# Two blocks on one core: shifted projections and output products in wide banks, the shift's mixing split over two engines, and sums moved

## The chip, the core and the metric

The kernel runs on one core of one Trainium2 chip. The metric is the device time of one execution in microseconds (us), lower is better. TensorE is PE in the rows, VectorE is DVE, ScalarE is ACT, GpSimd is POOL, SyncE is SP.

## The reference

Two blocks of two layers each run on 256 tokens of 1024 features, all in float32. Every layer is a feed-forward network, a mixer, and a second network. The change touches the mixers of the first block, and the place where every mixer hands over to its second network:

```python
h = rms_norm(x, mix_norm[layer])
p = h @ w_in
p_b = p[..., 4096:]
p_b = p_b + mu * (prev(p_b) - p_b)
r, k, v, w_down, a_down = split(p_b)
decay = f(w0 + tanh(w_down) @ w2)
a = sigmoid(a0 + a_down @ a2)
y_a = gated_spatial(p); y_b = time_mix(r, k, v, decay, a)
merged = sigmoid(gate_a) * (y_a @ w_proj_a) + sigmoid(gate_b) * (y_b @ w_proj_b)
x = x + merged @ w_out
```

Here prev(p) is p one token earlier, with zeros ahead of the first token.

## The kernel before

**Products.** Features lie on the 128 partitions, tokens (256) along the free axis. Each float32 operand is split into a high and a low part, and a product takes three terms: high by high, high by low, low by high. There are two forms. The narrow form (`three`, L2030 to L2034) issues three matmuls of 256 columns into one half of a PSUM bank of 512. The wide form (`unit_tiles`, L2122 to L2140) issues one matmul of 512 columns (the high weights against both parts of the activations, which lie side by side) and one of 256. It gives each tile a whole bank, whose two halves must then be added: ScalarE copies one half out, and VectorE adds the other. The networks use the wide form. The shifted projections and the output product of a mixer use the narrow one (`two_tiles`, L2036).

**Weights.** They come in units of 2048 columns, one DMA each, and a unit is 16 weight tiles, that is two halves of 8. ScalarE writes the high part of each half (L928), VectorE the low part (L1342). Both do so in `keep_ahead(w)`, called at fixed places of their programs: it splits all halves up to w + 3. There are four slots, so half m waits until TensorE is through with half m - 4.

**Order.** Each engine runs a program written out by hand, strictly in the order of its code, and waits on semaphores. `mixed` counts finished shift units, `emptied` the banks that ScalarE or VectorE have read, `tanh_ready` and others do what their names say. `bank_for` (L2019) hands out three narrow banks (`lin`, in rotation); `sv` has five more.

**The shift units.** In `rwkv(l)` a mixer starts with 13 units s = 0 to 12, each two tiles of p_b: the pair for decay and a (unit 0, tile `lora`), eight pairs of r and k, four pairs of v. The first two work on rough activations that are not normalized yet (`first_tiles`); the rest use h. For unit s:

- TensorE forms the products in a narrow bank.
- ScalarE calls `keep_ahead(base + 2 * s + 1)` and, from unit 2 on, copies the bank to `raw_shift` (L1068), which has two slots; for units 0 and 1 VectorE does that and scales by `rstd` (L1554). At s = 1 ScalarE also takes the tanh of `lora` (L1072), at s = 10 and 11 squares of the keys `kk` (L942).
- VectorE calls the same `keep_ahead`, then computes diff = prev - p (L1560) and p + mu * diff for each of the two tiles (L1569); from unit 9 on it also scales two tiles of keys into `kk` (L1574).

**After them.** TensorE forms z = tanh(w_down) @ w2 in four banks of `sv` (L2230), then a in four narrow banks (L2236). VectorE adds w0 to each bank of z into `decay` (L1581), ScalarE takes sigmoids of `decay` (L1079) and of a (L1083). A narrow bank can be taken again when the one three uses earlier is emptied. Then come the sums of the keys' squares (L2357) and the units of v_a and u_a.

**The end of a mixer.** Four output units d = 0 to 3 add to x (`residual`, L1516). While they run, ScalarE squares the finished parts of x (L942) and VectorE adds the first three of these into one (`add_squares`, L1379). TensorE turns them into the mean with matmuls against a constant (`norm_sums`, L2154): sum 0 right behind unit d = 3, sum 3 inside the first unit of the network, ahead of its tile k = 4.

## Time and profile before

| | us |
|---|---|
| median of 3 runs (lowest, highest) | 2853.32 (2848.67, 2853.98) |
| the profiled execution | 2854.39 |
| its span | 2852.7 |
| TensorE busy | 2771.2 (97%) |
| VectorE busy | 2127.5 (75%) |
| ScalarE busy | 1569.8 (55%) |
| share of the chain that ended last: TensorE, VectorE, ScalarE | 83%, 9%, 4% |

The profiled execution's own time is 1.7 us over its span, and 1.1 us over the median. Of a busy time it must be kept in mind that matmuls overlap: one of 256 columns is shown with 280 ns, while the next starts 120 ns after it. The start of one instruction to the start of the next is what a product costs. The granted TensorE clock was 0.995 of full speed over the whole span.

### The profile page before, as it was taken

To read this page: it belongs to the slowest core of one execution; us is meant where nothing else is said; L and a number is where in the kernel's file an instruction comes from. 1 tells how busy PE (TensorE), PEld (TensorE's weight loads), DVE (VectorE), ACT (ScalarE), POOL (GpSimd) and SP (SyncE) were. 2 spreads that over 40 slices of the span, in tenths; PEclk is the share of its full clock that TensorE was granted. 3 is DMA by queue.
4 is the path that set the end of the run, shared out by engine and by line. 5 is a ranking of instruction groups with operands and counts; after the bars stand their busy time and mean duration, and the time that the engine had idled before them with its cause. 6 is when DMAs were issued, how large, how long until landed. Compare 5 with 4: busy or idle time off the path is not lost.

```text
span 2852.7 us, 53213 instructions
## 1 busy us (share of the span) xinstructions
PE 2771.2 (97%) x22404; PEld 2469.4 (87%) x22404; DVE 2127.5 (75%) x3171; ACT 1569.8 (55%) x2377; POOL 13.8 (0%) x23
## 2 busy tenths in 40 slices
PE   7999999999999999999999999999999999998999
PEld 7889888898888898788988888888888879998888
DVE  7877667678788787666787798667878776777864
ACT  6545644455556455544465565576546546676653
POOL 0000000000000000000000000000000000000000
PEclk9999999999999999999999999899999999999999
DMA  6675311246757753111557567433675664332454
GB/s 232 250 280 179 131 46 47 88 162 227 266 211 253 286 180 133 61 46 46 193 202 260 203 246 259 178 119 128 249 269 212 246 234 165 146 134 104 163 183 142
DMA packets 72910, 510.62 MB, mean 179 GB/s; under 512 B 8480, under 2 KB 9248, under 8 KB 11872
## 3 DMA queue, kind: packets, MB, share of 16 engines
q1 hardware_dynamic: 72672, 507.22, 49.0%
q8 instruction: 177, 2.90, 0.4%
q14 instruction: 61, 0.50, 0.0%
HBM read 506.13 MB, written 1.05 MB: 178 GB/s over the span
## 4 chain that ended last, share of the span: by engine, by line
PE 83%; DVE 9%; ACT 4%; issue 2%; DMA 1%; SPq 0%; DVEq 0%; ACTq 0%
PE solve_banks L2135 13%; PE solve_banks L2198 11%; PE linear_banks L2135 7%; PE solve_banks L2136 7%; PE solve_banks L2199 6%; PE linear_banks L2032 5%; PE linear_banks L2033 4%; PE linear_banks L2034 4%; PE linear_banks L2136 4%; PE linear_banks L2587 3%; DVE split_halves L1342 3%; PE linear_banks L2588 3%; PE linear_banks L2589 3%; DMA raw_units<-in_stream 1%; PE solve_banks L2449 1%
## 5 line engine op out<-in xcount | busy, mean ns | idle before, releaser
L1342 DVE TENSOR_TENSOR split_halves<-raw_units,split_halves 128x1024 fp32r<-128x1024 f32 x806 | 971.9, 1221 | 315.8 <-ACT split_halves L928 313.2
L928 ACT ACTIVATE split_halves<-raw_units 128x1024 fp32r<-128x1024 f32 x806 | 841.4, 1054 | 437.1 <-PE solve_banks L2199 176.7
L2135 PE MATMUL solve_banks<-h_split,split_halves 128*128 128x512 f32 x1664 | 586.5, 397 | 1.4 <-DVE split_halves L1342 1.3
L2198 PE MATMUL solve_banks<-hidden_split,split_halves 128*128 128x512 f32 x1408 | 498.3, 398 | 0.6 <-DVE hidden_split L1452 0.6
L2136 PE MATMUL solve_banks<-h_split,split_halves 128*128 128x256 f32 x1664 | 465.5, 280 | 0.0
L2199 PE MATMUL solve_banks<-hidden_split,split_halves 128*128 128x256 f32 x1408 | 395.6, 281 | 0.0
L2135 PEld LDWEIGHTS solve_banks<-h_split,split_halves 128*128 128x128 f32 x1664 | 312.3, 188 | 77.5 <-issue 2.0
L2198 PEld LDWEIGHTS solve_banks<-hidden_split,split_halves 128*128 128x128 f32 x1408 | 264.7, 188 | 66.2 <-DVE hidden_split L1452 0.9
L2135 PE MATMUL linear_banks<-h_split,split_halves 128*128 128x512 f32 x896 | 317.3, 397 | 1.4 <-DVE split_halves L1342 1.0
L2136 PEld LDWEIGHTS solve_banks<-h_split,split_halves 128*128 128x128 f32 x1664 | 313.9, 189 | 0.0
L2032 PE MATMUL linear_banks<-h_split,split_halves 128*128 128x256 f32 x864 | 262.1, 303 | 5.7 <-DVE split_halves L1342 4.8
L2199 PEld LDWEIGHTS solve_banks<-hidden_split,split_halves 128*128 128x128 f32 x1408 | 264.3, 188 | 0.1
L2136 PE MATMUL linear_banks<-h_split,split_halves 128*128 128x256 f32 x896 | 250.8, 280 | 0.0
L2033 PE MATMUL linear_banks<-h_split,split_halves 128*128 128x256 f32 x864 | 244.8, 283 | 0.0
L2034 PE MATMUL linear_banks<-h_split,split_halves 128*128 128x256 f32 x864 | 244.4, 283 | 0.0
L2587 PE MATMUL linear_banks<-split_halves,h_split 128*128 128x256 f32 (+1 forms) x784 | 229.2, 292 | 9.6 <-DVE h_split L1421 9.4
L2588 PE MATMUL linear_banks<-split_halves,h_split 128*128 128x256 f32 (+1 forms) x784 | 224.0, 286 | 0.0
L2589 PE MATMUL linear_banks<-split_halves,h_split 128*128 128x256 f32 (+1 forms) x784 | 223.8, 286 | 0.0
L2135 PEld LDWEIGHTS linear_banks<-h_split,split_halves 128*128 128x128 f32 x896 | 168.2, 188 | 42.5 <-issue 2.1
L1446 DVE CUSTOM_DVE_ANT_0 raw_units<-raw_units,condition_rows,modulation 128x1024 f32<-128x1024 f32 x144 | 184.7, 1282 | 5.8 <-DMA raw_units<-in_mod_w 2.9
L2032 PEld LDWEIGHTS linear_banks<-h_split,split_halves 128*128 128x128 f32 x864 | 165.2, 191 | 18.8 <-issue 8.2
L2136 PEld LDWEIGHTS linear_banks<-h_split,split_halves 128*128 128x128 f32 x896 | 169.0, 189 | 0.0
(336 smaller groups left out, 4872.0 us busy)
## 6 DMA issues: line engine op xcount, KB each, us to landing
raw_units<-in_stream SPq DMA_DIRECT2D x403, 1024.0 KB, 4.8
raw_units<-in_mod_w SPq DMA_DIRECT2D x72, 1024.0 KB, 6.0
x<-in_x SPq DMA_DIRECT2D x4, 256.0 KB, 4.2
w2a<-in_w2a SPq DMA_DIRECT2D x2, 512.0 KB, 6.0
w_rows<-in_w SPq DMA_DIRECT2D x2, 512.0 KB, 8.0
bs_rows<-in_bs SPq DMA_DIRECT2D x2, 512.0 KB, 8.5
spatial_t<-in_ws_t SPq DMA_DIRECT2D x2, 512.0 KB, 10.4
out<-x SPq DMA_DIRECT2D x4, 256.0 KB, 4.3
```

What stands on the lines that cost most here:

```text
L928: nc.scalar.activation(split[:, n % SPLIT_SLOTS, 0, :], raw[:, item % RAW_SLOTS, (n % 2) * HALF * P:(n % 2 + 1) * HALF * P], ACT.Copy).the ...
L1342: V.tensor_tensor(split[:, n % SPLIT_SLOTS, 1, :], raw[:, item % RAW_SLOTS, (n % 2) * HALF * P:(n % 2 + 1) * HALF * P], split[:, n % SPLIT ...
L2032: M(o, w_hi, a_hi, start=start, stop=False, skip_group_check=skip)
L2033: M(o, w_hi, a_lo, start=False, stop=False, skip_group_check=skip)
L2034: return M(o, w_lo, a_hi, start=False, stop=stop, skip_group_check=skip)
L2135: M(pairs(banks[:, e, :]), s[:, 0, t], h[:, :, k, :], start=k == 0, stop=False)
L2136: ins = M(banks[:, e, 0:T], s[:, 1, t], h[:, 0, k, :], start=False, stop=k == DT - 1)
L2198: M(pairs(bank), s[:, 0, t], hidden[:, :, k, :], start=k == 0, stop=False)
L2199: ins = M(bank[:, 0:T], s[:, 1, t], hidden[:, 0, k, :], start=False, stop=k == FT - 1)
L2587: M(o, a_hi, s[:, 0, m], start=(c == 0 and j == 0), stop=False, skip_group_check=True)
L2588: M(o, a_lo, s[:, 0, m], start=False, stop=False, skip_group_check=True)
L2589: ins = M(o, a_hi, s[:, 1, m], start=False, stop=(c == DT - 1 and j == NCH - 1), skip_group_check=True)
```

## The change

Units 2 to 12 of the shift and the output units of the first block's mixers take the wide form. A new `pair_tiles` is the body of `unit_tiles`, with the banks as an argument; the shift units and the output units alternate between two pairs of banks of `sv`, so unit s waits for unit s - 2 to be emptied. The residual of such an output unit reads the two halves in two passes.

For a shift unit ScalarE copies the second half to `raw_shift`, and VectorE adds the first half to it. The mixing is written as mu * prev + (1 - mu) * p. ScalarE forms (1 - mu) * p in `diff` with two activations scaled by the new `one_less_mu`, and VectorE multiplies and adds in `mix(l, s)`, which it runs one unit later, behind the addition of unit s + 1. The tanh moves to s = 2. The banks of z are two of `sv` and two narrow ones, and the first bank of a has no wait.

Sum 0 of the four norms whose x comes from an output unit (two in each block) moves from behind unit d = 3 into the first unit of the network, just ahead of sum 3.

```diff
 for s in range(13):
-    p.use(("shift", l, s), "dve" if s < EARLY_UNITS else "act")
+    p.use(("shift", l, s), "dve")
 for s in range(4):
...
 u_ = over("u", [P, DT, T], 56)
+one_less_mu = over("one_less_mu", [P, 26], 66)
 bonus = v_first
...
 rest_copied = signal("rest_copied")
+shift_copied = signal("shift_copied")
+kept_ready = signal("kept_ready")
+less_ready = signal("less_ready")
 squares_added = signal("squares_added")
...
+def wide_banks(key):
+    kind, _, d = key
+    return down_banks(d) if kind == "down" else sv[:, 2 * (d % 2):2 * (d % 2) + 2, :]
+def shift_banks(s):
+    return sv[:, 2 * (s % 2):2 * (s % 2) + 2, :]
+def mix_out(s):
+    if s == 0:
+        return [(lora[:, 0, :], 24), (lora[:, 1, :], 25)]
+    if s < 9:
+        return [(r_[:, s - 1, :], s - 1), (k_[:, s - 1, :], 8 + s - 1)]
+    c = 2 * (s - 9)
+    return [(v_[:, c, :], 16 + c), (v_[:, c + 1, :], 17 + c)]
+def z_bank_of(l, s):
+    return sv[:, 2 + s, :] if s < 2 else lin[:, PLAN.uses["z", l, s][0] % 3, :]
 def x_wait(eng, n, i):
...
 if s >= EARLY_UNITS:
-    bank = wait_filled(act, ("shift", l, s))
+    wait_filled(act, ("shift", l, s))
     act.wait_ge(mixed, n - 1)
-    nc.scalar.activation(raw_shift[:, n % 2, :, 1:T + 1], pairs(bank), ACT.Copy)\
-        .then_inc(emptied["act"], 1)
-if s == 1:
+    nc.scalar.activation(raw_shift[:, n % 2, :, 1:T + 1], shift_banks(s)[:, :, T:2 * T], ACT.Copy)\
+        .then_inc(shift_copied, 1)
+if s == 0:
+    act.wait_ge(less_ready, l + 1)
+wait_emptied(act, ("shift", l, s))
+act.wait_ge(mixed, n)
+for i, (_, m) in enumerate(mix_out(s)):
+    ins = nc.scalar.activation(diff[:, i, :], raw_shift[:, n % 2, i, 1:T + 1], ACT.Copy,
+                               scale=one_less_mu[:, m:m + 1])
+ins.then_inc(kept_ready, 1)
+if s == 2:
     act.wait_ge(mixed, 13 * l + 1)
...
+def mix(l, s):
+    n = 13 * l + s
+    wait_emptied(dve, ("shift", l, s))
+    dve.wait_ge(kept_ready, n + 1)
+    for i, (o, m) in enumerate(mix_out(s)):
+        ins = V.scalar_tensor_tensor(o, raw_shift[:, n % 2, i, 0:T], col("mu", m, l), diff[:, i, :],
+                                     ALU.mult, ALU.add)
+    ins.then_inc(mixed, 1)
+    if s >= 9:
+        for c in (2 * s - 18, 2 * s - 17):
+            ins = V.tensor_scalar(kk[:, c, :], k_[:, c, :], col("k_k", c, l), None, ALU.mult)
+        ins.then_inc(kk_scaled, 1)
 def residual(key, c, factor, which):
     bank = pairs(wait_filled(dve, key))
-    if key[0] == "down":
+    if key[0] == "down" or key[1] < 2:
         for part in range(2):
-            both = down_banks(key[2])[:, :, part * T:(part + 1) * T]
+            both = wide_banks(key)[:, :, part * T:(part + 1) * T]
             if factor is not None:
...
 link(V.memset(raw_shift[:, :, :, 0:1], 0.0))
+mu = COL["mu", l]
+V.tensor_scalar(one_less_mu[:], cols[:, mu:mu + 26], -1.0, 1.0, ALU.mult, ALU.add)\
+    .then_inc(less_ready, 1)
 for s in range(13):
...
             .then_inc(emptied["dve"], 1)
-    wait_emptied(dve, ("shift", l, s))
-    if n:
-        dve.wait_ge(mixed, n)
-    b = raw_shift[:, n % 2, :, :]
-    link(V.tensor_tensor(diff[:], b[:, :, 0:T], b[:, :, 1:T + 1], ALU.subtract))
-    if s == 0:
-        dst = [(lora[:, 0, :], 24), (lora[:, 1, :], 25)]
-    elif s < 9:
-        dst = [(r_[:, s - 1, :], s - 1), (k_[:, s - 1, :], 8 + s - 1)]
     else:
-        c = 2 * (s - 9)
-        dst = [(v_[:, c, :], 16 + c), (v_[:, c + 1, :], 17 + c)]
-    for i, (o, m) in enumerate(dst):
-        ins = V.scalar_tensor_tensor(o, diff[:, i, :], col("mu", m, l), b[:, i, 1:T + 1],
-                                     ALU.mult, ALU.add)
-    ins.then_inc(mixed, 1)
-    if s >= 9:
-        for c in (2 * s - 18, 2 * s - 17):
-            ins = V.tensor_scalar(kk[:, c, :], k_[:, c, :], col("k_k", c, l), None, ALU.mult)
-        ins.then_inc(kk_scaled, 1)
+        wait_filled(dve, ("shift", l, s))
+        dve.wait_ge(shift_copied, (13 - EARLY_UNITS) * l + s - EARLY_UNITS + 1)
+        V.tensor_tensor(raw_shift[:, n % 2, :, 1:T + 1], shift_banks(s)[:, :, 0:T],
+                        raw_shift[:, n % 2, :, 1:T + 1], ALU.add).then_inc(emptied["dve"], 1)
+    if s:
+        mix(l, s - 1)
+mix(l, 12)
 dve.wait_ge(mixed, 13 * l + 13)
...
     wait_filled(dve, ("z", l, s))
-    V.tensor_tensor(decay[:, s // 2, (s % 2) * 512:(s % 2 + 1) * 512], sv[:, s, :],
+    V.tensor_tensor(decay[:, s // 2, (s % 2) * 512:(s % 2 + 1) * 512], z_bank_of(l, s),
                     w0_b[:, (s % 2) * 512:(s % 2 + 1) * 512], ALU.add).then_inc(emptied["dve"], 1)
...
 if k == 4:
-    for m in (0, 3) if n == 0 else (3,):
+    for m in (0, 3) if n == 0 or X_FROM[n][0] == "out" else (3,):
         for a in norms_in(n):
...
         wait_emptied(pe, ("gu", i, j - 3))
+    elif i in (1, 3):
+        if j < 2:
+            wait_emptied(pe, (*X_FROM[ffn_norm(i)], j + 2))
+        elif i == 1:
+            wait_emptied(pe, ("vback", 0, VALUES_BACK[3][-1]))
     elif i and j:
...
     unit_free(i, j)
-    banks = unit_banks(i, j)
+    pair_tiles(w, unit_banks(i, j), ready)
+def pair_tiles(w, banks, ready=None):
     order = [(e, k) for k in range(DT) for e in range(2)] if ready else \
...
     norm_sums(n, d - 1)
-elif d == 3:
+elif d == 3 and key[0] == "down":
     norm_sums(n, 0)
...
     else:
-        two_tiles(base + 2 * s, ("shift", l, s), (HH, HH),
-                  h_wait(3 * l + 1) if s == EARLY_UNITS else None)
+        wait_emptied(pe, ("shift", l, s - 2) if s > EARLY_UNITS + 1 else ("down", 2 * l, 3))
+        pair_tiles(base + 2 * s, shift_banks(s), h_wait(3 * l + 1) if s == EARLY_UNITS else None)
 pe.wait_ge(consts_loaded, 16)
...
     j = s // 2
-    M(sv[:, s, :], lora[0:64, 0, j * CH:(j + 1) * CH], w2a2[0:64, (s % 2) * 512:(s % 2 + 1) * 512],
+    wait_emptied(pe, ("shift", l, 11 if s < 2 else 1))
+    M(z_bank_of(l, s), lora[0:64, 0, j * CH:(j + 1) * CH], w2a2[0:64, (s % 2) * 512:(s % 2 + 1) * 512],
       start=True, stop=True).then_inc(lin_filled, 1)
 for s in range(4):
-    bank = bank_for(("a", l, s))
+    bank = bank_for(("a", l, s)) if s else lin[:, PLAN.uses["a", l, 0][0] % 3, :]
     for i in range(2):
...
 for d in range(4):
-    two_tiles(OUT_AT[l] + 2 * d, ("out", l, d), (HH, HH),
-              (lambda k: pe.wait_ge(merged_split, 4 * l + k // 2 + 1)) if d == 0 else None)
+    if d >= 2:
+        wait_emptied(pe, ("out", l, d - 2))
+    pair_tiles(OUT_AT[l] + 2 * d, wide_banks(("out", l, d)),
+               (lambda k: pe.wait_ge(merged_split, 4 * l + k // 2 + 1)) if d == 0 else None)
     early_sums(("out", l), d)
```

ScalarE, shift units 0 to 2 of the first layer. Lines of the changed kernel are numbered anew: L954 is the split, L1094 the copy, L1101 the two scales, L1106 the tanh. Before:

```order
L928 ACTIVATE split_halves<-raw_units 128x1024 [waits halves_used,raw_loaded_1]
L1072 ACT_TABLE_LOAD
L1072 ACTIVATE lora<-lora 64x256 [waits mixed]
L928 ACTIVATE split_halves<-raw_units 128x1024 [waits lin_filled,raw_loaded_1]
L928 ACTIVATE split_halves<-raw_units 128x1024 [waits halves_used,raw_loaded_2]
L1068 ACTIVATE raw_shift<-linear_banks 128x2x256 [waits mixed,lin_filled]
L928 ACTIVATE split_halves<-raw_units 128x1024 [waits lin_filled,raw_loaded_2]
L928 ACTIVATE split_halves<-raw_units 128x1024 [waits halves_used,raw_loaded_0]
```

Now:

```order
L1101 ACTIVATE diff<-raw_shift,one_less_mu 128x256 [waits mixed,emptied_by_dve,less_ready]
L1101 ACTIVATE diff<-raw_shift,one_less_mu 128x256
L954 ACTIVATE split_halves<-raw_units 128x1024 [waits halves_used,raw_loaded_1]
L1101 ACTIVATE diff<-raw_shift,one_less_mu 128x256 [waits mixed,emptied_by_dve]
L1101 ACTIVATE diff<-raw_shift,one_less_mu 128x256
L954 ACTIVATE split_halves<-raw_units 128x1024 [waits lin_filled,raw_loaded_1]
L954 ACTIVATE split_halves<-raw_units 128x1024 [waits halves_used,raw_loaded_2]
L1094 ACTIVATE raw_shift<-solve_banks 128x2x256 [waits mixed,lin_filled]
L1101 ACTIVATE diff<-raw_shift,one_less_mu 128x256 [waits mixed,emptied_by_dve]
L1101 ACTIVATE diff<-raw_shift,one_less_mu 128x256
L1106 ACT_TABLE_LOAD
L1106 ACTIVATE lora<-lora 64x256 [waits mixed]
```

The tanh went behind unit 2. Two scales stand between the splits of one unit and the next, and their waits name `mixed` and `emptied_by_dve`.

VectorE, the same units (L1376 is the split, L1605 and L1610 write `raw_shift`, L1556 mixes). Before:

```order
L1554 TENSOR_TENSOR raw_shift<-linear_banks,rstd 128x2x256 [waits lin_filled,dve_step]
L1560 TENSOR_TENSOR diff<-raw_shift 128x512 [waits emptied_by_dve]
L1569 SCALAR_TENSOR_TENSOR lora<-diff,columns,raw_shift 128x256 [waits dve_step]
L1569 SCALAR_TENSOR_TENSOR lora<-diff,columns,raw_shift 128x256
L1342 TENSOR_TENSOR split_halves<-raw_units,split_halves 128x1024 [waits hi_ready]
L1554 TENSOR_TENSOR raw_shift<-linear_banks,rstd 128x2x256 [waits lin_filled]
L1560 TENSOR_TENSOR diff<-raw_shift 128x512 [waits mixed,emptied_by_dve]
L1569 SCALAR_TENSOR_TENSOR r<-diff,columns,raw_shift 128x256 [waits dve_step]
L1569 SCALAR_TENSOR_TENSOR k<-diff,columns,raw_shift 128x256
```

Now:

```order
L1598 TENSOR_SCALAR one_less_mu<-columns 128x26 [waits dve_step]
L1605 TENSOR_TENSOR raw_shift<-linear_banks,rstd 128x2x256 [waits lin_filled]
L1376 TENSOR_TENSOR split_halves<-raw_units,split_halves 128x1024 [waits hi_ready]
L1605 TENSOR_TENSOR raw_shift<-linear_banks,rstd 128x2x256 [waits lin_filled]
L1556 SCALAR_TENSOR_TENSOR lora<-raw_shift,columns,diff 128x256 [waits kept_ready,emptied_by_dve]
L1556 SCALAR_TENSOR_TENSOR lora<-raw_shift,columns,diff 128x256
L1376 TENSOR_TENSOR split_halves<-raw_units,split_halves 128x1024 [waits hi_ready] x2
L1610 TENSOR_TENSOR raw_shift<-solve_banks,raw_shift 128x2x256 [waits shift_copied,lin_filled]
L1556 SCALAR_TENSOR_TENSOR r<-raw_shift,columns,diff 128x256 [waits kept_ready,emptied_by_dve]
L1556 SCALAR_TENSOR_TENSOR k<-raw_shift,columns,diff 128x256
```

The subtraction is gone, an addition that waits for ScalarE's copy has come, and the mixing of a unit follows the write of the next unit.

TensorE, z and the first banks of a (L2278 and L2284 now). Before:

```order
L2230 MATMUL solve_banks<-w2a_91,lora 128x512 [waits tanh_ready,small_loaded,consts_loaded]
L2230 MATMUL solve_banks<-w2a_91,lora 128x512 x3
L2236 MATMUL linear_banks<-lora,w2a_91 128x256 [waits emptied_by_dve]
L2236 MATMUL linear_banks<-lora,w2a_91 128x256
L2236 MATMUL linear_banks<-lora,w2a_91 128x256 [waits emptied_by_dve]
L2236 MATMUL linear_banks<-lora,w2a_91 128x256
```

Now:

```order
L2278 MATMUL solve_banks<-w2a_92,lora 128x512 [waits tanh_ready,emptied_by_dve,small_loaded,consts_loaded]
L2278 MATMUL solve_banks<-w2a_92,lora 128x512 [waits emptied_by_dve]
L2278 MATMUL linear_banks<-w2a_92,lora 128x512 [waits emptied_by_dve] x2
L2284 MATMUL linear_banks<-lora,w2a_92 128x256 x2
L2284 MATMUL linear_banks<-lora,w2a_92 128x256 [waits emptied_by_dve]
L2284 MATMUL linear_banks<-lora,w2a_92 128x256
L2284 MATMUL linear_banks<-lora,w2a_92 128x256 [waits emptied_by_dve]
```

The matmuls of z now wait for emptied banks, the first bank of a waits for nothing, and the second still waits for VectorE.

## Rows read from the trace of the kernel before

**Rows 1.** The page, costliest groups: line, engine, operation, tiles, count, busy us, mean ns.

```profile
L928 ACT ACTIVATE split_halves<-raw_units 128x1024 fp32r<-128x1024 f32 x806 | 841.4, 1054 | 437.1 <-PE solve_banks L2199 176.7
```

**Rows 2.** Waits of PE, whole span: waiting line, releaser, us in total, times, longest.

```profile
PE solve_banks L2154 <- DVE squares L1379: 6.1, 4, 2.4
```

**Rows 3.** Timeline of ScalarE, shift units: start us, us, line, operation, tiles, idle and releaser.

```profile
239.18 0.60 ACT L1068 ACTIVATE raw_shift<-linear_banks 128x512 f32<-128x512 f32 x1 [1.76 <-PE linear_banks L2034]
...
244.94 0.60 ACT L1068 ACTIVATE raw_shift<-linear_banks 128x512 f32<-128x512 f32 x1 [1.76 <-PE linear_banks L2034]
```

**Rows 4.** Timeline of VectorE, network 0, two units of the 512-column kind.

```profile
65.27 0.69 DVE L1468 TENSOR_TENSOR unit_sums<-solve_banks,unit_sums 128x512 f32<-128x512 f32 x1 [1.00 <-ACT unit_sums L1039]
...
70.92 0.69 DVE L1468 TENSOR_TENSOR unit_sums<-solve_banks,unit_sums 128x512 f32<-128x512 f32 x1 [0.64 <-ACT unit_sums L1039]
```

**Rows 5.** Timeline of VectorE, first shift units of layer 0.

```profile
223.35 0.69 DVE L1554 TENSOR_TENSOR raw_shift<-linear_banks,rstd 128x512 f32<-128x512 f32 x1
...
228.98 2.35 DVE L1342 TENSOR_TENSOR split_halves<-raw_units,split_halves 128x1024 fp32r<-128x1024 f32 x2
...
231.25 0.69 DVE L1560 TENSOR_TENSOR diff<-raw_shift 128x512 f32<-128x512 f32 x1
```

**Rows 6.** Timeline of ScalarE, the same stretch.

```profile
223.53 1.28 ACT L1072 ACT_TABLE_LOAD   x1
...
225.71 0.42 ACT L1072 ACTIVATE lora<-lora 64x256 f32<-64x256 f32 x1 [0.90 <-DVE lora L1569]
...
226.04 1.99 ACT L928 ACTIVATE split_halves<-raw_units 128x1024 fp32r<-128x1024 f32 x2
```

**Rows 7.** Timeline of VectorE, last shift unit and the first sums of z.

```profile
286.62 0.88 DVE L1569 SCALAR_TENSOR_TENSOR v<-diff,columns,raw_shift 128x256 f32<-128x256 f32 x2
...
287.41 0.61 DVE L1574 TENSOR_SCALAR kk<-k,columns 128x256 f32<-128x256 f32 x2
...
287.94 2.48 DVE L1581 TENSOR_TENSOR decay<-solve_banks,w_rows 128x512 f32<-128x512 f32 x4
```

**Rows 8.** Timeline of ScalarE: a scale by a column, and squares of the keys.

```profile
622.23 0.90 ACT L1005 ACTIVATE rough_split<-x,columns 128x256 fp32r<-128x256 f32 x2
...
623.03 0.19 ACT L954 ACTIVATE table_probe<-constants 128x1 f32<-128x1 f32 x1
...
274.24 0.62 ACT L942 ACTIVATE squares<-kk 128x512 f32<-128x512 f32 x1
...
274.76 1.05 ACT L928 ACTIVATE split_halves<-raw_units 128x1024 fp32r<-128x1024 f32 x1
```

**Rows 9.** Timeline of PE, z, a and the key sums of layer 0.

```profile
285.15 3.70 PE L2230 MATMUL solve_banks<-w2a,lora 64*128 64x512 f32 x8
...
289.28 3.72 PE L2236 MATMUL linear_banks<-lora,w2a 64*128 64x256 f32 x16 [0.43 <-DVE decay L1581]
...
292.92 1.90 PE L2357 MATMUL linear_banks<-squares,constants 128*16 128x256 f32 x8
```

**Rows 10.** End of the output product of layer 0: VectorE, ScalarE, PE.

```profile
624.02 0.68 DVE L1379 TENSOR_TENSOR squares<-squares 128x512 f32<-128x512 f32 x1
...
624.63 0.68 DVE L1534 SCALAR_TENSOR_TENSOR x<-linear_banks,x 128x512 f32<-128x512 f32 x1
...
625.34 0.63 ACT L942 ACTIVATE squares<-x 128x512 f32<-128x512 f32 x1 [2.13 <-DVE x L1534]
...
624.76 1.13 PE L2154 MATMUL solve_banks<-squares,constants 128*128 128x256 f32 x4 [1.24 <-DVE squares L1379]
```

**Rows 11.** Idle PE and its clock: PE's timeline, and stretches (PEclk third from the end).

```profile
2347.19 0.55 PE L2587 MATMUL linear_banks<-split_halves,h_split 128*128 128x256 f32 x1 [4.49 <-DVE h_split L1421]
...
2350.00:2351.00 1.00, 0.57 (x4) 0.44 (x4) 0.96 (x3) 0.61 (x2) 0.00 (x0) 0.94 0.00 0
...
1814.22 0.35 PE L2587 MATMUL linear_banks<-split_halves,h_split 128*128 128x16 f32 x1 [4.02 <-DVE h_split L1421]
...
1826.00:1828.00 2.00, 2.00 (x12) 2.00 (x12) 1.70 (x4) 1.45 (x3) 0.00 (x0) 0.53 0.00 0
```

## The prediction

> **What bounds the kernel now.** I read the page first: TensorE is busy for 97% of the span and carries 83% of the chain that ended last. So a change pays if it takes TensorE's time, and it costs whenever VectorE or ScalarE come so late that TensorE stands. The list of PE's waits then says where it stands today. In the shift stages it hardly does. At the four hand-overs from an output product to a network it waits 6.1 us in all for the added squares [rows 2]. Last, the timelines of ScalarE and VectorE tell how much room they have in a shift unit. TensorE finishes one every 5.76 us (the copies start at 239.18 and 244.94), and ScalarE idles 1.76 us ahead of each copy [rows 3]. That room is what the change spends.
>
> **Wide products.** A network's unit has the same 16 weight tiles in the wide form, and its additions start 5.65 us apart (65.27, 70.92) [rows 4]. So a unit gets 5.76 - 5.65 = 0.11 us shorter on TensorE, not a third: one matmul in three goes, but its columns stay. Eight output units save 0.9 us. Twenty-two shift units would save 2.4 us, if TensorE still set their pace. The Trainium skill ("TensorE: Matmul & The Clock Gate", "Wait — 56ns, not 53.3ns?") says that a warm matmul costs its columns at 2.4 GHz and some 2.5 ns. By this rule, an estimate, 16 tiles with one matmul less save 0.04 us, 30 units 1.2 us where the rows give 3.3 us. The rows decide here.
>
> **The loop of a shift unit.** Now the other two engines, for which I add up one unit, from the start of VectorE's addition for unit s to the same for s + 1. Each step waits for the one ahead of it:
>
> - VectorE adds (0.61 us to the next start, as between 624.02 and 624.63 [rows 10]) and mixes unit s - 1 (0.88 us for two [rows 7]): 1.49 us.
> - ScalarE may write `diff` only once that mixing has read it, so its two scales start 0.04 us later. They take 0.80 us to the next start, like the scale by a column at 622.23 [rows 8]: 2.33 us.
> - Only then come its splits. The first takes 1.05 us [rows 1] and VectorE can follow 0.04 us later: 3.42 us.
> - VectorE's two low parts take 2.27 us to the next start (228.98 to 231.25) [rows 5]: 5.69 us.
>
> ScalarE's second split and its copy fit beside the low parts. The loop's 5.69 us are 0.04 us over TensorE's new 5.65 us. In the kernel before no such loop exists: ScalarE splits and copies without waiting for VectorE's mixing of the same unit, and time lost is made up. Now nothing is made up, and everything that falls into the loop stays.
>
> **From the first write of `raw_shift` to the first addition of z.** Before: 223.35 [rows 5] to 287.94 [rows 7], 64.59 us. After:
>
> - 0.1 us for `one_less_mu`, ahead of everything.
> - Unit 0 to unit 1, with one split and no mixing: 0.69 + 0.04 + 0.80 + 1.05 + 0.04 + 1.13 = 3.75 us.
> - Eleven loops: 62.59 us.
> - The tanh at unit 2 with its table load, today in idle time, now in the loop: 1.28 + 0.33 = 1.61 us [rows 6].
> - Two squares of keys, also in the loop: 2 x 0.52 = 1.04 us (274.24 to 274.76) [rows 8].
> - The end: addition and mixing of unit 11 (1.49), 0.04, scales of unit 12 (0.89), 0.04, its mixing (0.80) and its keys (0.53, 287.41 to 287.94 [rows 7]): 3.79 us.
>
> Together 72.9 us, 8.3 us more. TensorE is hit twice. Inside the stage it stands at the second halves of units 3 and 4 (1.6 us each, as the low part of half 7 comes at 231.9, not 230.2), and it ends its last unit near 288.1 where it now starts z at 285.15 [rows 9]. That alone would be 3 us, but it is hidden behind the second: after z (3.70 us) and the free first bank of a it needs the third bank of z emptied, 1.93 us behind the first addition of z, which comes at 296.3. Three banks of a (0.93 us each) later TensorE is 4.8 us behind that addition; today it is 5.0 us behind (292.92, where the key sums start) [rows 9]. So the stage costs 8.3 - 0.2 = 8.1 us. Behind it TensorE, ScalarE and VectorE are all late by the same, TensorE sets the pace again, and no row offers slack that takes it back. Two layers: **+16.2 us**. Bounds for a layer: +1.4 us (only the late mixing of unit 12, all else hidden) and +10 us (each of twelve handovers 0.15 us slower than I took it). I take the sum, since every term has its own row.
>
> **The clock.** TensorE then stands about 5.2 us at one stretch (293.0 to 298.2). In the kernel before, an idle time of 4.49 us ended at 2347.19 with the granted clock at 1.2 GHz instead of 2.4 (a matmul of 256 columns takes 0.55 us). It was back at 2350, after 2.9 us of dense work, which lost 1.4 us. Behind an idle time of 4.02 us that ended at 1814.22 the clock was low until about 1827.9, so 13.7 us of work lost 6.8 us [rows 11]. Ours is dense work behind a similar idle time, so I take the first: **+2.8 us** for two layers; bounds 0 and +13.6 us.
>
> **The sums.** TensorE now waits 1.24 us for the last added squares and then works on tiles 0 to 3 of the first unit before it needs sum 3 [rows 10]. With sum 0 behind these tiles (2.9 us of work) the wait is covered: the squares are added at 624.7, TensorE arrives near 626. Next late is the square of the last part of x. In the first block the residual takes two passes instead of one (0.7 us more), so the square ends at 626.7 instead of 625.97 [rows 10], about when sum 0 is done. So nearly all of the four waits goes, and I keep 0.9 us back for rough parts of tile 6 and h that become the next wait: 6.1 - 0.9 = **-5.2 us** (bounds -3, if half of them turns into such waits, and -6.1).
>
> **VectorE's other extras.** The second pass of the eight output residuals lies in the idle time that VectorE has there (a quarter of the span); if that cover were gone, 8 x 0.7 = 5.6 us. The double buffer costs nothing there: unit d waits for the residual of d - 2, which has the whole 5.65 us of unit d - 1 to run in. DMAs are neither added nor moved; a weight unit is requested up to 7 us later in the loop, but it has two units' time in hand.
>
> **Sum.** 16.2 + 2.8 - 0.9 - 5.2 = +12.9 us on the profiled execution's 2854.39, that is 2867.3; the median of the runs is 1.1 us lower, so **2866.2 us**. About 0.2% (5.7 us) is what a measurement of this kernel can tell from no change.
>
> **The rivals.**
>
> - *TensorE keeps the pace* (0.14). If ScalarE's scales or the handovers are a little faster than their rows, the loop is under 5.65 us and lateness is made up as it is today. Then -3.3 (30 units), -5.2 (sums) and +2 x 1.4 for the late mixing of unit 12: 2847.6 us. For it speaks that the loop is only 0.04 us over; against it that tanh, table load and the first units are in the loop in any case, and that the loop must fall below by 0.4 us a unit to make those up. The point from which it decides is a loop of about 5.3 us. By the skill's price of a matmul, again an estimate, it would be 2849.7 us.
> - *Half of it is made up* (0.14). With a loop of 5.4 us a layer gains 11 x 0.29 = 3.2 us back, the idle time shrinks to 2 us and the clock stays: 2 x 4.9 - 6.1 = +3.7 us, 2857.0 us.
> - *The clock stays low for long* (0.12). As at 1827.9: 6.8 us instead of 1.4 us a layer, 2877.0 us.
> - *The clock does not fall.* Then 2863.4 us; this is inside my forecast (0.60 with it).
>
> **Chances and range.** The forecast and the long low clock are slower by more than 0.2% (0.72), with a little from the upper part of the third case (0.02). The made-up half and most of the first rival are within 0.2% (0.19). The rest of the first rival, with all waits of the sums gone, is faster (0.07). The range takes in the forecast with its bounds, the half made up and the long clock, and leaves out the first rival: 2855 to 2878. The forecast's own range is 2860 to 2872.
>
> **What would show it.** Right: VectorE's additions to `raw_shift` (L1610) start 5.7 us apart, the one around the tanh 7.3 us; ScalarE shows waits for the mixing ahead of its scales (L1101); TensorE waits for low parts at units 3 and 4 and over 4 us ahead of the second bank of a (L2284); from the first `raw_shift` to `decay` some 73 us; the waits of the sums (L2201) for added squares near 0. Wrong: spacing of 5.65 us with VectorE idle ahead of each addition, `decay` starting at 290 or earlier, or output units that TensorE can't start because a residual is late.

## The result, and the profile after

The changed kernel takes 2880.05 us (median of 4 runs, 2876.79 to 2882.93) where the kernel before takes 2853.57 (4 runs): ratio 1.0089, 95% interval 1.0074 to 1.0103. That is 26.5 us slower. The prediction said slower by 12.9 us, range up to 2878. Of a later run of another kernel the ratio is what counts, since the median of the kernel before moved between 2852.0 and 2857.5 us from one set of runs to the next.

| | before | changed |
|---|---|---|
| profiled execution, its span | 2854.39, 2852.7 | 2881.4, 2879.7 |
| granted clock over the span | 0.995 | 0.989 |
| TensorE, VectorE, ScalarE busy | 2771.2, 2127.5, 1569.8 | 2782.8, 2128.8, 1592.9 |

The page of the changed kernel, its chain by engine:

```profile
PE 79%; DVE 12%; ACT 5%; issue 3%; DMA 1%; SPq 0%; ACTq 0%; DVEq 0%
```

TensorE lost 4 points of the chain, VectorE won 3. TensorE's waits, whole span (waiting line, releaser, us in total, times, longest):

```profile
PE linear_banks L2284 <- DVE decay L1620: 12.8, 2, 6.4
PE solve_banks L2182 <- DVE split_halves L1376: 12.2, 13, 1.7
PE linear_banks L2182 <- DVE split_halves L1376: 4.5, 4, 1.5
PE solve_banks L2201 <- ACT squares L968: 3.7, 3, 1.7
```

Two new waits of 6.4 us stand ahead of the second bank of a, and the wait for added squares [rows 2] is gone. The next two lines, waits for VectorE's low parts, add up to 16.7 us. The lines of the wide form had 2.3 us before, but the shift and output units, which run through them now, had lines of their own then. In e1, a version without the loop that is described next, they add up to 9.2 us.

**The shift.** VectorE's timeline, two units of layer 0 (start us, us, line, operation, tiles, idle and releaser):

```profile
243.19 0.69 DVE L1610 TENSOR_TENSOR raw_shift<-solve_banks,raw_shift 128x512 f32<-128x512 f32 x1
243.80 0.48 DVE L1556 SCALAR_TENSOR_TENSOR r<-raw_shift,columns,diff 128x256 f32<-128x256 f32 x1
244.19 0.48 DVE L1556 SCALAR_TENSOR_TENSOR k<-raw_shift,columns,diff 128x256 f32<-128x256 f32 x1
246.66 2.36 DVE L1376 TENSOR_TENSOR split_halves<-raw_units,split_halves 128x1024 fp32r<-128x1024 f32 x2 [1.99 <-ACT split_halves L954]
248.94 0.69 DVE L1610 TENSOR_TENSOR raw_shift<-solve_banks,raw_shift 128x512 f32<-128x512 f32 x1
```

and ScalarE's:

```profile
244.76 0.91 ACT L1101 ACTIVATE diff<-raw_shift,one_less_mu 128x256 f32<-128x256 f32 x2 [2.45 <-DVE k L1556]
245.58 2.00 ACT L954 ACTIVATE split_halves<-raw_units 128x1024 fp32r<-128x1024 f32 x2
247.47 0.57 ACT L1094 ACTIVATE raw_shift<-solve_banks 128x512 f32<-128x512 f32 x1
```

VectorE's second row and its third are the mixing of the unit before. Read in turn, this is the loop: addition 243.19, scales 244.76, ScalarE's split 245.58, VectorE's splits 246.66, addition 248.94. It takes 5.74 us, and both engines idle in it, each for the other: ScalarE 2.45 us, VectorE 1.99 us. From the first write of `raw_shift` (220.45) to the first sum of z (294.03) it is 73.58 us where [rows 5, 7] give 64.59.

**The wait and the clock behind it.** TensorE's timeline, layer 0, then layer 1:

```profile
288.58 1.02 PE L2278 MATMUL linear_banks<-w2a,lora 64*128 64x512 f32 x2
295.97 5.48 PE L2284 MATMUL linear_banks<-lora,w2a 64*128 64x256 f32 x12 [6.37 <-DVE decay L1620]
301.38 2.94 PE L2407 MATMUL linear_banks<-squares,constants 128*16 128x256 f32 x8
304.25 0.39 PE L2117 MATMUL linear_banks<-split_halves,h_split 128*128 128x256 f32 x1
```

```profile
1104.86 5.48 PE L2284 MATMUL linear_banks<-lora,w2a 64*128 64x256 f32 x12 [6.41 <-DVE decay L1620]
1110.27 7.19 PE L2292 MATMUL linear_banks<-lora,v 32*128 32x256 f32 x16
1117.39 3.60 PE L2407 MATMUL linear_banks<-squares,constants 128*16 128x256 f32 x8
1120.91 0.58 PE L2117 MATMUL linear_banks<-split_halves,h_split 128*128 128x256 f32 x1
```

In the kernel before, the second of these rows was

```profile
1089.21 3.72 PE L2244 MATMUL linear_banks<-lora,v 32*128 32x256 f32 x16
```

So the same 16 small matmuls of the gate of v took 3.72 us before and 7.19 us now. Stretches of layer 1 say why (the granted clock is third from the end):

```profile
1106.00:1110.00 4.00, 4.00 (x11) 2.84 (x9) 0.00 (x0) 2.48 (x7) 0.00 (x0) 0.50 0.00 0
...
1119.00:1122.00 3.00, 3.00 (x10) 1.54 (x9) 2.83 (x6) 1.55 (x3) 0.00 (x0) 0.50 0.00 0
```

TensorE ran at 1.2 GHz from about 1102.2 to 1122.7 us, and in layer 0 from 293.3 to 303.5. I count as *work lost* the busy time of TensorE times (1 - granted clock), summed over stretches of 1 us: 8.9 and 3.8 us. Over the whole span it is 24.3 us, and 9.9 in the kernel before. The Trainium skill ("TensorE: Matmul & The Clock Gate", Terms) prices a throttled stretch at half its length; by that rule, an estimate, the 16.1 us of layer 1 from the end of the wait to v_a cost 8.0 us. The trace agrees within 0.5 us: at full clock the same matmuls take 3.0 us (the 12 of a, in e3) and 5.5 us (1089.21 to 1094.69 in the kernel before), 7.5 us less. My work lost is built on that same half, so it tells how long TensorE worked at 1.2 GHz and is no second proof of the price.

All that follows is read at three points of a mixer: the first `raw_shift`, the first sum of z (`decay`), and the first matmul of v_a (L2117; before, L2078 at 294.75 and 1094.69 us). In the table, "to decay" is the time from the first to the second point, "to v_a" from the second to the third, and "wait" is what TensorE waits between z and v_a.

| kernel | ratio to before (95%) | layer 0: to decay, to v_a (wait) | layer 1: to decay, to v_a (wait) |
|---|---|---|---|
| before | 1 | 64.59, 6.81 (0.43) | 64.60, 10.46 (0.42) |
| changed | 1.0089 (1.0074 to 1.0103) | 73.58, 10.22 (6.37) | 73.59, 17.98 (6.41) |
| e1 mixing on VectorE | 1.0002 (0.9992 to 1.0013) | 63.38, 10.76 (1.82) | 64.39, 12.10 (1.82) |
| e2 two buffers | 1.0036 (1.0025 to 1.0047) | 66.47, 10.88 (3.05) | 67.16, 16.85 (2.83) |
| e3 wait filled | 1.0043 (1.0029 to 1.0056) | 73.57, 6.80 (1.3, 0.3) | 73.56, 12.09 (1.3, 0.3) |
| e4 sums alone | 0.9995 (0.9985 to 1.0005) | 64.59, 6.81 (0.42) | 64.60, 13.79 (0.43) |
| e5 e1, wait filled | 0.9968 (0.9956 to 0.9980) | 64.39, 6.81 (0) | 64.40, 12.03 (0) |
| e6 e1, own banks for a | 0.9947 (0.9934 to 0.9959) | 64.40, 3.77 (0) | 64.40, 12.36 (0.96) |
| e7 z before last mixing | 1.0048 (1.0034 to 1.0062) | 71.58, 10.61 (4.37) | 71.58, 17.51 (4.37) |
| e8 splits before scales | 0.9997 (0.9987 to 1.0006) | 64.39, 10.87 (2.95) | 63.31, 17.99 (2.95) |
| e9 e8, own banks for a | 0.9976 (0.9967 to 0.9986) | 64.38, 3.77 (0.77) | 63.23, 12.12 (0.77, 1.80) |
| e10 changed, own banks | 1.0053 (1.0037 to 1.0069) | 73.56, 5.90 (1.26, 1.84) | 73.59, 13.38 (1.32, 1.16) |
| e11 before, other waits | 1.0019 (1.0009 to 1.0029) | 64.60, 7.70 (2.02) | 64.60, 15.47 (2.02) |
| e12 e6, attention filled | 0.9972 (0.9960 to 0.9983) | 64.38, 3.77 (0) | 63.39, 12.36 (0.80) |

The changed kernel's extra is +9.0 us a layer up to decay, and +3.4 and +7.5 us from there to v_a: 28.9 us. The rest takes 2 to 3 us off. The ratios come from five sets of runs (changed; e1 to e4; e5 to e8; e9 to e11; e12), and each is taken against the kernel before in its own set.

### The profile page after: what moved, and what is told of

Its sections match the earlier page's. It is cut to its first block, busy times and chain, and to the rows that moved or that the text cites. A ratio compares the mean times of both kernels' runs of the same rounds, so it can differ in the third digit from the quotient of the medians.

```text
span 2879.7 us, 52357 instructions
## 1 busy us (share of the span) xinstructions
PE 2782.8 (97%) x21924; PEld 2450.5 (85%) x21924; DVE 2128.8 (74%) x3177; ACT 1592.9 (55%) x2429; POOL 15.6 (1%) x23
## 3 DMA queue, kind: packets, MB, share of 16 engines
q8 instruction: 173, 2.83, 0.4%
## 4 chain that ended last, share of the span: by engine, by line
PE 79%; DVE 12%; ACT 5%; issue 3%; DMA 1%; SPq 0%; ACTq 0%; DVEq 0%
PE solve_banks L2182 14%; PE solve_banks L2245 11%; PE linear_banks L2182 7%; PE solve_banks L2183 7%; PE solve_banks L2246 6%; DVE split_halves L1376 4%; PE linear_banks L2183 4%; PE linear_banks L2071 3%; PE linear_banks L2637 3%; PE linear_banks L2638 3%; PE linear_banks L2639 3%; PE linear_banks L2072 2%; PE linear_banks L2073 2%; ACT split_halves L954 1%; PE solve_banks L2499 1%
## 5 line engine op out<-in xcount | busy, mean ns | idle before, releaser
L1376 DVE TENSOR_TENSOR split_halves<-raw_units,split_halves 128x1024 fp32r<-128x1024 f32 x806 | 971.2, 1222 | 354.6 <-ACT split_halves L954 352.8
L954 ACT ACTIVATE split_halves<-raw_units 128x1024 fp32r<-128x1024 f32 x806 | 840.3, 1053 | 405.1 <-PE solve_banks L2246 186.8
L2182 PE MATMUL solve_banks<-h_split,split_halves 128*128 128x512 f32 x2144 | 760.1, 398 | 12.6 <-DVE split_halves L1376 12.2
L2183 PE MATMUL solve_banks<-h_split,split_halves 128*128 128x256 f32 x2144 | 600.9, 280 | 0.0
L2182 PEld LDWEIGHTS solve_banks<-h_split,split_halves 128*128 128x128 f32 x2144 | 402.4, 188 | 116.1 <-DVE split_halves L1376 13.4
L2183 PEld LDWEIGHTS solve_banks<-h_split,split_halves 128*128 128x128 f32 x2144 | 404.7, 189 | 0.0
L2183 PE MATMUL linear_banks<-h_split,split_halves 128*128 128x256 f32 x896 | 251.0, 280 | 0.0
L2182 PEld LDWEIGHTS linear_banks<-h_split,split_halves 128*128 128x128 f32 x896 | 168.2, 188 | 46.2 <-issue 4.1
L2183 PEld LDWEIGHTS linear_banks<-h_split,split_halves 128*128 128x128 f32 x896 | 169.2, 189 | 0.0
L2637 PEld LDWEIGHTS linear_banks<-split_halves,h_split 128*128 128x128 f32 x784 | 154.1, 197 | 15.1 <-issue 11.6
L2638 PEld LDWEIGHTS linear_banks<-split_halves,h_split 128*128 128x128 f32 x784 | 154.3, 197 | 0.0
L2639 PEld LDWEIGHTS linear_banks<-split_halves,h_split 128*128 128x128 f32 x784 | 154.2, 197 | 0.0
L1065 ACT ACTIVATE unit_sums<-solve_banks 128x512 f32<-128x512 f32 x104 | 62.1, 597 | 130.6 <-PE solve_banks L2183 130.6
```

Of the source, the lines that this page charges most:

```text
L954: nc.scalar.activation(split[:, n % SPLIT_SLOTS, 0, :], raw[:, item % RAW_SLOTS, (n % 2) * HALF * P:(n % 2 + 1) * HALF * P], ACT.Copy).the ...
L1065: nc.scalar.activation(units[:, n % 3, :, :], unit_banks(i, j)[:, :, T:2 * T], ACT.Copy)\
L1376: V.tensor_tensor(split[:, n % SPLIT_SLOTS, 1, :], raw[:, item % RAW_SLOTS, (n % 2) * HALF * P:(n % 2 + 1) * HALF * P], split[:, n % SPLIT ...
L2182: M(pairs(banks[:, e, :]), s[:, 0, t], h[:, :, k, :], start=k == 0, stop=False)
L2183: ins = M(banks[:, e, 0:T], s[:, 1, t], h[:, 0, k, :], start=False, stop=k == DT - 1)
L2637: M(o, a_hi, s[:, 0, m], start=(c == 0 and j == 0), stop=False, skip_group_check=True)
```

## The experiments

**e1 and e8: is it the loop?** The theory: the scales stand ahead of the splits on ScalarE and wait for VectorE. The rival: the wide form, or simply too much work. e1 puts the mixing back as it was:

```diff
-wait for the mixing of s - 1; two scales on ScalarE
 VectorE: add unit s
-mix(l, s - 1): mu * prev + kept
+mix(l, s):     diff = prev - p; p + mu * diff
```

> The changed kernel with the mixing put back to VectorE (subtraction, then two multiply-adds, right behind the addition of the same unit) and the tanh back at unit 1; wide products, output units and moved sums stay. Theory (the loop ScalarE scales wait for VectorE's mixing, then ScalarE's splits, then VectorE's splits is the cost): a unit of VectorE is 2.27 + 0.61 + 0.73 + 0.80 = 4.4 us against TensorE's 5.65 us, no loop, no idle time of 6.4 us ahead of the second bank of a, clock stays at 2.4 GHz there: 2853.6 - 2.4 (22 shift units) - 0.9 (output units) - 2 (sums, as the changed kernel's trace shows) + 1 (sums of z a little later) = about 2849 us. First raw_shift to first decay 64 us or less (64.59 before, 73.58 in the changed kernel). Rival (the two bank pairs of the wide form hold TensorE, or the copy and addition of a wide unit come too late): still above 2870 us and over 70 us from raw_shift to decay.

Ratio 1.0002: all 0.9% are gone, with the wide products still in. The table shows the same: both mixers together, up to v_a, are 24.7 us shorter than in the changed kernel. The additions come 5.55 us apart in layer 0 and 5.65 in layer 1. But the hoped-for gain did not come either: TensorE now waits 1.82 us, and the clock falls behind that too (5.0 us of work lost in layer 0).

e8 leaves every instruction of the change in place and swaps two calls on ScalarE:

```diff
+    if s < 12:
+        keep_ahead(base + 2 * s + 3)
     wait_emptied(act, ("shift", l, s))
     act.wait_ge(mixed, n)
     ...two scales...
```

> The changed kernel with ScalarE's splits for the next unit put ahead of the scales of this one; one buffer for the scaled p as before, the same instructions. Theory (the loop closes only because ScalarE's splits stand behind scales that wait for VectorE's mixing): no loop is left, VectorE's additions come 5.55 to 5.65 us apart with VectorE idle ahead of them, also at the tanh and the squares of the keys; raw_shift to the first sum of z about 65.5 us instead of 73.6; what stays is the late mixing of unit 12 (1.4 us a layer) and a clock that may fall as it did with two buffers: ratio about 1.002 (2861 us beside 2855.7). Rival (too much work for one unit on ScalarE or VectorE): spacing near 5.74 us and ratio 1.008.

VectorE's timeline of e8:

```profile
264.58 0.69 DVE L1612 TENSOR_TENSOR raw_shift<-solve_banks,raw_shift 128x512 f32<-128x512 f32 x1 [1.14 <-ACT raw_shift L1094]
...
270.24 0.69 DVE L1612 TENSOR_TENSOR raw_shift<-solve_banks,raw_shift 128x512 f32<-128x512 f32 x1 [1.15 <-ACT raw_shift L1094]
...
275.89 0.69 DVE L1612 TENSOR_TENSOR raw_shift<-solve_banks,raw_shift 128x512 f32<-128x512 f32 x1 [1.15 <-ACT raw_shift L1094]
```

VectorE idles 1.15 us ahead of each addition and TensorE sets the pace, also around the squares of the keys (270.24 to 275.89). Up to decay both layers are as early as in the kernel before (64.39 and 63.31 us), with every instruction of the change still there. So the delay of the loop came from the order of two calls; the amount of work, the wide banks and the copy are excluded as its cause.

The ratio of 0.9997 says more than that and must not be put down to the swap alone. Up to v_a the two mixers are 18.8 us shorter than in the changed kernel, while the ratio falls by some 26 us; and they are 10.1 us longer than in the kernel before, since the wait of 2.95 us and its low clock are still there (26.1 us of work lost over the span). The rest lies in stages that the swap does not touch; the last section has a part of it.

**e2: the loop by its other link.** A second buffer for the scaled p (`diff` for even, `diff_odd` for odd units; the scales wait for `mixed` n - 1).

> The changed kernel with two buffers for the scaled p: ScalarE's scales of unit s wait for VectorE's addition of unit s alone and no longer for the mixing of unit s - 1. Not one instruction's work is less. Theory (the wait on the one buffer closes the loop): the loop falls by the mixing, 5.74 - 0.88 = 4.9 us, under TensorE's 5.65 us, so TensorE sets the pace, time lost at the tanh and the squares is made up, and only the late mixing of unit 12 stays (+1.4 us a layer, clock unhurt): about 2853.6 - 2.4 - 0.9 - 2 + 2.8 = 2851 us, raw_shift to decay about 66 us. Rival (ScalarE and VectorE have too much work in a unit, whatever the order): stays at 2880 us with 73.6 us.

```profile
247.88 0.68 DVE L1612 TENSOR_TENSOR raw_shift<-solve_banks,raw_shift 128x512 f32<-128x512 f32 x1
...
250.48 2.36 DVE L1378 TENSOR_TENSOR split_halves<-raw_units,split_halves 128x1024 fp32r<-128x1024 f32 x2 [1.14 <-ACT split_halves L956]
252.76 0.68 DVE L1612 TENSOR_TENSOR raw_shift<-solve_banks,raw_shift 128x512 f32<-128x512 f32 x1
```

The loop is 4.88 us, the forecast 4.9, and lateness is made up by unit 8. But at 1.0036 the time is some 13 us above what I expected. The squares and keys of the last units lie in the loop again (5.93 us a unit), so z's sums come late, TensorE waits 3.05 us, and the clock falls for 5.0 and 6.8 us of work. The mechanism was right, the remaining wait was priced without its clock.

**e3 and e5: what does the clock cost?** 20 matmuls of 512 columns that nobody reads stand in the changed kernel's wait:

```diff
+if s == 0:
+    wait_emptied(pe, ("shift", l, 12))
+    for q in range(20):
+        M(pairs(sv[:, 0, :]), h[:, 0, q % 8, 0:P], h[:, :, q % 8, :], start=True, stop=True)
```

> The changed kernel with 20 matmuls of 512 columns whose result nobody reads, in the wait of TensorE ahead of the second bank of a (behind the emptied banks of unit 12, about 290.8 us in layer 0); the chain of the other engines is as it was. Theory (the clock, and not the 6.4 us of waiting alone, costs what the forecast missed): the granted clock stays at 2.4 GHz to 304 and at 334 us in layer 0 and from 1102 to 1123 us in layer 1, and the time falls by about the work lost there, 3.8 + 1.7 + 8.9 = 14.4 us at most, of which some stays since ScalarE's sigmoids and VectorE's sums pace the banks of a too: 2880 - 10 = 2870 us. Rival (that work is paced by the other engines, the clock costs only the forecast's 2.8 us): 2877 us. If the time does not change, the clock costs nothing.

TensorE's timeline and two stretches of e3:

```profile
290.14 4.81 PE L2290 MATMUL solve_banks<-h_split 128*128 128x512 f32 x20 [1.26 <-DVE raw_shift L1610]
295.24 3.11 PE L2284 MATMUL linear_banks<-lora,w2a 64*128 64x256 f32 x12 [0.29 <-DVE decay L1620]
298.28 1.90 PE L2411 MATMUL linear_banks<-squares,constants 128*16 128x256 f32 x8
```

```profile
293.00:296.00 3.00, 2.71 (x13) 1.97 (x12) 2.97 (x8) 2.16 (x5) 0.00 (x0) 1.00 0.00 0
296.00:300.00 4.00, 4.00 (x18) 2.10 (x16) 0.07 (x1) 3.95 (x10) 0.00 (x0) 1.00 0.01 4
```

The chain is untouched (73.57 us), the clock stays at 2.4 GHz (in layer 1 until 1103.3 us, then 1.7 us of work are lost), and in layer 0 the 12 matmuls of a take 3.11 us instead of 5.48. From decay to v_a it is 6.80 us, as before the change. The ratio falls from 1.0089 to 1.0043, about 13 us, of which the table shows 9.3 (3.4 and 5.9). So the clock costs a third to a half of the loss, three to five times my +2.8 us. It also answers what ScalarE's sigmoids do: they don't pace this stretch.

e5 does the same to e1, with 7 matmuls in its wait of 1.82 us.

> The run with the mixing back on VectorE, plus 7 matmuls of 512 columns that nobody reads, in TensorE's wait of 1.8 us ahead of the second bank of a. In that run the wide units came 5.54 us apart in layer 0 (5.65 in layer 1), but the granted clock fell to 1.2 GHz from 285.3 to 295.7 us and 5.0 us of work were lost, where the kernel before loses none. Theory (the small matmuls of z and a with a wait among them let the clock fall, a wait of 1.8 us is enough for it): the clock stays at 2.4 GHz in layer 0 until v_a, -5 us in layer 0 and -1.7 us in layer 1 against that run: ratio about 0.998, 2849 us where the kernel before has 2855. Rival (the clock falls there whatever TensorE does, or the fall costs nothing because ScalarE's sigmoids pace the banks): ratio 1.000 as without them.

Layer 0 goes from 10.76 back to 6.81 us, as expected; layer 1 hardly moves (12.10 to 12.03), since a later dip of 1.7 us stays. The ratio is 0.9968, faster than the kernel before. Its gain over e1 is larger than the 4 us that the mixers' traces show behind decay; on that, see the last section.

**e7: the end of the chain.** VectorE's sums of z ahead of the mixing of unit 12.

> The changed kernel with VectorE's four sums of z ahead of the mixing of unit 12 instead of behind it. Theory (the chain add 12, mix 11, scales 12, mix 12, keys, sums of z ends TensorE's wait): the sums of z start 2.0 us earlier (0.58 wait, 0.80 mixing, 0.52 keys, and 0.04), the wait ahead of the second bank of a falls from 6.4 to 4.4 us in both layers, -4 us: 2876 us, ratio 1.0075 against 1.0089; if the shorter wait also spares the clock, up to 14 us less, ratio 1.003. Rival (the squares of the last keys, which come later now, become the wait ahead of their sums): ratio unchanged.

To decay 71.58 us, 2.0 less; the wait 4.37, 2.0 less; both to 0.05 us. The clock fell all the same. The ratio is 1.0048, 12 us under the changed kernel's, where the mixers' traces show 4.1: the larger part is not explained by this edit (for some of it see the last section).

**e6, e9, e10: taking the wait away.** In e1, the second and third bank of a take the pair of shift unit 12, the fourth z's first bank:

```diff
+def a_bank_of(l, s):
+    return sv[:, s - 1, :] if s else lin[:, PLAN.uses["a", l, 0][0] % 3, :]
-bank = bank_for(("a", l, s)) if s else lin[:, PLAN.uses["a", l, 0][0] % 3, :]
+bank = a_bank_of(l, s)
+if s:
+    wait_emptied(pe, ("shift", l, 12) if s < 3 else ("z", l, 0))
```

and the next three narrow banks wait for z's third and fourth bank and a's first.

> The run with the mixing back on VectorE, and other banks for a: the second and third bank of a take the pair of shift unit 12, the fourth the first bank of z, and the sums of the keys and the first banks behind them wait for z's banks and a's first instead of a's others. No work is added or left out. Theory: TensorE's waits of 1.8 us (two times) ahead of the second bank of a go, z and a run on without a gap, so the clock need not fall in layer 0 (5.0 us of work) and 1 (1.7 us): 2857 - 3.6 - 6.7 = 2847 us beside 2855.7 of the kernel before, ratio 0.997. Rival (the next wait, for ScalarE's squares of the keys behind the sigmoids, takes their place and the clock falls all the same): ratio 1.000.

```profile
285.65 2.32 PE L2286 MATMUL solve_banks<-lora,w2a 64*128 64x256 f32 x10
287.95 1.90 PE L2409 MATMUL linear_banks<-squares,constants 128*16 128x256 f32 x8
289.78 0.39 PE L2117 MATMUL linear_banks<-split_halves,h_split 128*128 128x256 f32 x1
```

TensorE runs from z to v_a without a gap, 3.77 us from decay instead of 6.81. Ratio 0.9947: **this version beats both kernels**. But the two mixers up to v_a account for 1.5 us of that against the kernel before. The profiled executions differ by 12.2 us. From one stage's last residual to the next one's, 9.4 of these lie in the four networks of the first block; three of the four have a faster pace here, worth some 6.6 us (last section). e12, which contains this version, has 0.9972. So its gain is 0.3 to 0.5%. What the banks give is read against e1, which differs by them alone: the mixers up to v_a are 5.7 us shorter.

In layer 1 a wait of 0.96 us in v's gate remains, and 4.6 us of work are lost. But the clock did not fall behind that wait:

```profile
1077.22 3.95 PE L2294 MATMUL linear_banks<-lora,v 32*128 32x256 f32 x12
1082.13 2.07 PE L2294 MATMUL linear_banks<-lora,v 32*128 32x256 f32 x4 [0.96 <-ACT pair L1123]
```

```profile
1079.00:1080.00 1.00, 1.00 (x3) 0.70 (x3) 0.00 (x0) 1.00 (x4) 0.00 (x0) 0.68 0.00 0
1080.00:1081.00 1.00, 1.00 (x3) 0.34 (x2) 0.00 (x0) 1.00 (x4) 0.00 (x0) 0.50 0.00 0
```

The clock fell at about 1079.4, ahead of the wait (1081.2 to 1082.1), after TensorE had run the small matmuls of z, a and the gate for 7.7 us without a gap. e12 shows the same: the clock fell at 1073.3, and the wait began at 1075.9.

> The run with ScalarE's splits ahead of the scales (mixing on both engines as in the change), with the other banks for a. Alone, the early splits gave 0.9997 of the kernel before: TensorE still waited 2.95 us ahead of the second bank of a, and in its trace 4.9 + 1.7 + 8.4 + 1.7 = 16.7 us of work were lost to the low clock behind z and a. Theory (what the change still loses there is that wait and the clock that falls with it): the wait goes, most of the clock with it, -10 to -18 us: 2840 to 2846 us beside 2856, ratio 0.9945 to 0.9965, as good as the run with the mixing on VectorE. Rival (the late mixing of unit 12 now holds the sums of the keys or v_a, so a wait of 1.4 us or more stays and the clock falls all the same): ratio 0.999.

With the mixing on both engines, the early splits and these banks the ratio is 0.9976, a gain, but short of the 0.9945 to 0.9965 I expected. In the mixers' traces the two are 1.4 us apart (143.5 and 144.9 us up to v_a), and the comparison of the ratios is one across sets. So I can show no gain of splitting the mixing over two engines against leaving it to VectorE.

> The changed kernel itself, with the other banks for a and nothing else. The shift's chain stays at 73.6 us, so VectorE's sums of z start 4.5 us behind TensorE's first bank of a as before, and TensorE still has to wait for the first of them (fourth bank of a) and for the third (sums of the keys). Theory (TensorE is held by the chain, the banks decide only how the wait is cut): some 2 us a layer less waiting, and the clock falls as before: ratio about 1.007. Rival (the single bank wait is the whole cost, the loop of the shift is hidden): ratio under 1.000.

For the change itself the banks cut the one wait of 6.4 us into 1.26 and 1.84 us; 1.0053. The loop still costs what it did (73.56 us). Its stretch to v_a (5.90 and 13.38 us, from 10.22 and 17.98) gained more than my 2 us a layer.

**e11: the same idea in the kernel before.**

```diff
+if key[0] == "a" and key[2] < 3:
+    wait_emptied(pe, ("shift", key[1], (11, 12, 10)[key[2]]))
-if n >= 3:
+elif n >= 3:
```

> The kernel before, where the first three banks of a wait for shift units 10 to 12 alone and no longer for the sums of z (no instruction added or left out). It tells whether the gain of the run with own banks for a (0.9947) is the banks' or the wide units'. Theory (the kernel before waits only 0.43 us there and its clock does not fall, so there is little to win): -1 to -2 us, ratio 0.9995, and the gain of that run is that of the wide units and moved sums once the wait they uncover is gone. Rival (the banks would give the same to any version): ratio 0.996 or less.

Both expectations missed: it is slower, 1.0019 (1.0009 to 1.0029). TensorE, and its clock behind the wait:

```profile
291.37 1.13 PE L2238 MATMUL linear_banks<-lora,w2a 64*128 64x256 f32 x4 [2.02 <-ACT a L1083]
292.42 2.79 PE L2359 MATMUL linear_banks<-squares,constants 128*16 128x256 f32 x8
```

```profile
292.00:294.00 2.00, 2.00 (x9) 0.79 (x8) 0.00 (x0) 1.89 (x6) 0.00 (x0) 0.82 0.00 0
294.00:297.00 3.00, 3.00 (x12) 2.00 (x11) 0.01 (x1) 1.81 (x3) 0.00 (x0) 0.55 0.00 0
```

Three banks went early and the fourth waits for a's sigmoid: 2.02 us at one stretch in place of 0.43 us [rows 9]. The clock fell in both layers (1.7 and 5.1 us of work lost). So starting three banks of a early does not pay by itself. What differs in e6 is that the fourth bank needs no sigmoid either, so no such wait is left. The full bank plan of e6 was not tried in the kernel before, nor were the wide units tried apart from it, so this run does not say how much of e6's gain is whose.

**e4: the sums alone**, in the kernel before.

> The kernel before with the moved sums alone: sum 0 of the four norms whose x comes from an output unit goes ahead of sum 3 in the first unit of the network. Theory by the changed kernel's trace (VectorE's split for the first unit of h becomes the next wait): the waits of 6.1 us for added squares go, and about 4 us come back ahead of unit 2: -2 us, 2851.5 us, and TensorE's L2135 waits for split_halves grow from 2.3 us to about 5. The forecast's term: -5.2 us, 2848.4 us.

Ratio 0.9995: the interval reaches to -4.3 us and leaves the forecast's -5.2 out. From the end of the last output unit to the first unit of h, the traces give 1.2, 1.3, 1.1 and 0.3 us less at the four hand-overs, 3.9 us together. What took the rest stands in TensorE's timeline of e4, at the last two:

```profile
1978.11 0.47 PE L2135 MATMUL linear_banks<-h_split,split_halves 128*128 128x512 f32 x1 [0.95 <-DVE split_halves L1342]
```

```profile
2657.87 0.36 PE L2032 MATMUL solve_banks<-rough_split,split_halves 128*128 128x258 f32 x1 [0.30 <-DVE split_halves L1342]
...
2662.20 1.13 PE L2154 MATMUL solve_banks<-squares,constants 128*128 128x256 f32 x4 [0.36 <-ACT squares L942]
```

The wait moved to VectorE's low part for the first unit of h, which stands behind the residual and the root of the norm. In the changed kernel, with its two residual passes in the first block, the four hand-overs give 0.4, 0.6, 1.1 and 0.3 us: 2.5 us together before rounding.

**e12: are such waits worth filling anywhere?** In e6, 8 and 9 unread matmuls stand in the waits at the start of the two attention layers, those of [rows 11].

> The run with own banks for a (ratio 0.9947), with 8 and 9 matmuls of 256 columns that nobody reads in TensorE's waits of 4.0 and 4.5 us at the start of the two attention layers, which the change does not touch and every version has. In that run 7.0 us of work were lost to the low clock behind the first (1799 to 1817 us) and 1.4 us behind the second. Theory (a wait of some 2 us or more that TensorE spends idle makes the clock fall, and dense work that starts again brings it back only much later where it is itself broken by waits): the clock stays at 2.4 GHz at both places, -7 to -8.4 us, 2834 us beside 2857, ratio 0.9920. Rival (what counts is the work around the wait, not the idle time, or the lost work lay beside the other engines' chain): ratio 0.9947 as without.

```profile
2327.87 4.05 PE L2565 MATMUL solve_banks<-constants 128*128 128x256 f32 x18
2332.53 0.36 PE L2642 MATMUL linear_banks<-split_halves,h_split 128*128 128x256 f32 x1 [0.61 <-DVE h_split L1452]
```

The clock stayed up in the second layer, and in the first it fell 7 us later behind the root of that norm (5.0 us of work lost instead of 7.0). But from VectorE's reciprocal of that root to the next norm's the trace gives 156.8 us and 319.8 us, in e6 157.1 and 319.8: at most 0.3 us gained. The low clock had lain beside VectorE's chain of h, whose waits of 0.6, 0.3 and 1.1 us came up in its place. The rival was right. The ratio is 0.9972, even above that of e6. Most of that is the kernel before, which had a median of 2851.99 us in this set and 2857.46 in that of e6; the two versions' own medians are 2844.06 and 2841.82 us. So a ratio of one set carries some 0.2% more doubt than its interval says when it is held against one of another set. A gain of the filling is not shown.

## Why the prediction was right and wrong

**Right: the direction and the mechanism.** The step "the loop of a shift unit" held in each term. Addition to scales 1.57 us (forecast 1.53), scales to split 0.82 (0.80), split to low parts 1.08 (1.09), low parts to addition 2.28 (2.27): 5.74 against 5.69. The unit around the tanh took 7.47 us (forecast 7.30), the squares 0.52 each as forecast. e8 shows the cause: with the same instructions and no loop, decay comes as early as in the kernel before.

**Small miss: first `raw_shift` to `decay`.** 73.6 us against 72.9, so +9.0 a layer against +8.3; twelve handovers each some hundredths slower. TensorE stood at the second halves of units 3 and 4 as forecast, 1.49 and 1.65 us against 1.6 each, and once more for 0.82 us, at the start of unit 3. Its wait ahead of the second bank of a was 6.4 us where I had 5.2. Nor were 0.2 us hidden behind the banks: at full clock decay to v_a is the same 6.8 us (e3). The step says +16.2 for two layers; it was +18.0.

**Wrong: the step "the clock", +2.8 us.** I took the first row of [rows 11], 1.4 us a layer, because "ours is dense work behind a similar idle time". It is not dense: a, the gate of v and the sums of the keys are small matmuls, and the clock stayed at 1.2 GHz through all of them in layer 1 and nearly all in layer 0. On the path from decay to v_a that cost +3.4 us in layer 0 and +7.5 in layer 1, 10.9 together, near the upper bound (13.6) that I had from the second row. The rival "the clock stays low for long" (0.12, 2877.0 us) was the nearest of all; e3 confirms the price. Choosing between two rows I looked at the wait ahead and not at what TensorE runs behind it. The rows themselves held the hint: behind the short dip stood matmuls of 256 columns, behind the long one those of 16 (128x16 in [rows 11]).

**Wrong: the step "the sums", -5.2 us.** The waits went as forecast, but I kept back only 0.9 us for the next wait. That one took 2.2 of the 6.1 us back in e4, and 3.6 in the changed kernel, where two residual passes stand ahead of two of the four: -2.5 us.

**Right by the unit, half in the sum: the output units.** TensorE's first output product starts at 611.10 and what follows the last at 634.00 us, 22.90 us against 23.09 before, and layer 1 gives the same: -0.2 us in four units, -0.4 for eight; forecast -0.9. From one unit to the next it is the 0.11 us of the forecast, but the first unit takes 0.14 us longer. The shift units gained nothing, as forecast; without the loop one is 5.55 or 5.65 us.

Together: 18.0 + 10.9 - 0.4 - 2.5 = +26.0 us. The spans differ by 27.0, the medians by 26.5. That they agree so well is in part luck: by the last residual of each stage, the first network of the profiled execution is 3.1 us shorter than in the kernel before and the second block 2.8 us longer, and the change touches neither the one nor, but for two moved sums, the other.

## What to carry to other kernels

Before moving work to an idle engine, look at what stands behind it in that engine's program: a wait on the other engine, placed ahead of work that this other engine needs, closes a loop in which both idle, and swapping two calls (e8) took out all of its delay. Price a wait of TensorE with the work behind it: where small matmuls followed, the low clock cost between half of the wait and two and a half times the wait on top; one wait of 2 us can be dearer than a short one (e11), and filling it helps only if no other engine's chain runs beside it. A wait that is removed at a hand-over is worth only its distance to the next one.

## What I had not expected of the hardware

- **How short a wait is enough.** The granted clock fell behind waits of 1.82 us (e1) and 2.02 us (e11), each amid small matmuls: 0.1 us behind the end of the wait in layer 0 of e1, but 6.5 us behind it in layer 1. Behind 0.42 to 0.43 us at the same place it stayed up in three of four cases; in layer 1 of e4, whose shift code is that of the kernel before, it fell nonetheless (3.4 us of work lost), 5.4 us behind the wait. And in layer 1 of e6 and e12 it fell ahead of any wait, after 7 to 8 us of small matmuls without a gap. So a wait is not needed for it. In layer 1 of the kernel before, 13 us of them with one wait of 0.42 us left the clock up. What decides between the two stays open.
- **Dips behind next to no wait.** Some 3.4 us at 1.2 GHz stand behind the small matmuls that spread the keys' norms, with waits of 0.3 and 0.15 us among them: from 334.2 us in the changed kernel, from 1124.7 in the kernel before. The stretch below begins ahead of the fall, so its clock is a mean of both levels:

```profile
334.00:336.00 2.00, 2.00 (x11) 1.86 (x10) 0.94 (x1) 0.00 (x0) 0.00 (x0) 0.56 0.22 29
```

- **Two paces of the same products.** A unit of 16 tiles in the wide form takes 5.65 us in some stages and 5.54 in others, at a granted clock of 1.00 in both: in the second network the kernel before and the changed one had 5.65, e6 had 5.54. In e1 layer 0 had the fast pace and layer 1 the slow one, in e8 the other way round. A network's stage differs by 2.2 us with it. I have no cause for it. It is part of why executions of one kernel spread over 10 us or more, and why the gains of e5 to e8 in the ratio are larger than what their mixers' traces show: all four are of one set, and the kernel before had its highest median in that set (2857.46 us). Of the eight stages of the networks, two had the fast pace in the profiled executions of the kernel before and of the changed one, three in e5, four in e6 and e8, five in e7 and six in e12, the shortest of all (2835.1 us). At 2.2 us a stage that is 2 to 9 us. What decides the pace stays open.
